# Parameter rows on ScalarE's queue, x without a pause on SyncE's, and two dense steps between the last transposes of x

## The reference

```
def rmsnorm(x, g):
    y = x * rsqrt(mean(x * x, axis=-1) + EPS)
    return y * g

for i in range(DEPTH):                      # 2 layers
    h = rmsnorm(x, norm_g[i])
    proj = einsum('bsd,dn->bsn', h, w_in[i])
    (qa, ka, va, fa, za, qb, kcb, ...) = split_cols(proj)
    ...                                     # three mixers, merge, residual, embedding
return rmsnorm(x, final_g)
```

## Time and profile before

| | |
|---|---|
| median of three runs | 1510.43 us (1510.29 to 1510.44) |
| profiled execution, its own time | 1511.0 us |
| its span, first to last instruction | 1509.1 us |
| mean granted TensorE clock | 0.995 |
| PE busy | 1477.2 us, 98% of the span |
| DVE busy | 938.5 us, 62% |
| ACT busy | 634.6 us, 42% |

### The profile page before, as it was taken

One profiled execution on the slowest core, in us unless ns is written; L12 is line 12 of the kernel. 1 busy time (PEld: TensorE's weight loads), 2 busy tenths in 40 slices (PEclk: granted clock), 3 DMA queues, 4 the chain that ended last, 5 costly groups with the idle time before them and its releaser, 6 DMA issues.

```text
span 1509.1 us, 22243 instructions
## 1 busy us (share of the span) xinstructions
PE 1477.2 (98%) x7765; PEld 1226.0 (81%) x7765; DVE 938.5 (62%) x2197; ACT 634.6 (42%) x1499; POOL 75.8 (5%) x79
## 2 busy tenths in 40 slices
PE   7999999999999999999999999999999999999997
PEld 6777788888888887888787887888888888878885
DVE  5866765655657776454576667655555666855544
ACT  5544434434344344243444434334344444434343
POOL 1000000000001000000100000000000000000011
PEclk9999999999999999999999999999999999999998
DMA  6325353224325543332342345423343355433222
GB/s 188 85 80 124 107 123 78 71 71 112 78 64 139 140 119 85 110 102 70 109 110 70 104 100 129 116 57 78 79 99 82 98 126 127 111 99 104 84 88 74
DMA packets 259262, 150.48 MB, mean 100 GB/s; under 512 B 47482, under 2 KB 247764, under 8 KB 259156
## 3 DMA queue, kind: packets, MB, share of 16 engines
q1 hardware_dynamic: 259156, 149.11, 38.1%
HBM read 118.67 MB, written 2.10 MB: 80 GB/s over the span
## 4 chain that ended last, share of the span: by engine, by line
PE 82%; DVE 8%; ACT 3%; issue 3%; DMA 2%; SPq 1%; POOL 0%; ACTq 0%; POOLq 0%; DVEq 0%
PE D L774 22%; PE D L776 21%; PE D L775 21%; PE Ob L965 7%; PE T L943 4%; DVE w_lo L1329 3%; PE S L930 2%; PE S L931 2%; ACT w_hi L1095 1%; PE S L920 1%; DMA arena<-rcs 1%; PE Mb L981 1%; ACT probs L1207 1%; DVE v_b L1424 1%; PE Ob L969 1%
## 5 line engine op out<-in xcount | busy, mean ns | idle before, releaser
L774 PE MATMUL D<-h_hi,w_hi 128*128 128x512 f32 x1264 | 539.0, 426 | 3.5 <-DVE w_lo L1329 1.7
L1329 DVE TENSOR_TENSOR w_lo<-raw,w_hi 128x512 fp32r<-128x512 f32 (+2 forms) x504 | 296.3, 628 | 322.8 <-ACT w_hi L1095 322.5
L776 PE MATMUL D<-h_lo,w_hi 128*128 128x512 f32 x1264 | 496.9, 393 | 0.0
L775 PE MATMUL D<-h_hi,w_lo 128*128 128x512 f32 x1264 | 494.9, 392 | 0.0
L1095 ACT ACTIVATE w_hi<-raw 128x512 fp32r<-128x512 f32 (+2 forms) x504 | 263.6, 569 | 291.4 <-PE D L776 287.9
L776 PEld LDWEIGHTS D<-h_lo,w_hi 128*128 128x128 f32 x1264 | 237.6, 188 | 53.4
L1207 ACT ACTIVATE probs<-probs,nmax 128x128 f32<-128x128 f32 (+3 forms) x256 | 141.9, 555 | 330.0 <-DVE nmax L1580 329.9
L774 PEld LDWEIGHTS D<-h_hi,w_hi 128*128 128x128 f32 x1264 | 239.2, 189 | 47.5 <-issue 6.6
L775 PEld LDWEIGHTS D<-h_hi,w_lo 128*128 128x128 f32 x1264 | 239.9, 190 | 30.4 <-issue 0.5
L1580 DVE CUSTOM_DVE_ANT_0 probs<-S,maskb 128x128 f32<-128x128 f32 (+3 forms) x256 | 115.2, 487 | 26.2 <-PE S L923 12.8
L556 DVE COPY pT<-T 128x128 f32<-128x128 f32 (+3 forms) x160 | 77.6, 487 | 55.1 <-PE T L943 54.5
(11 more groups left out here) (249 smaller groups left out, 1596.2 us busy)
## 6 DMA issues: line engine op xcount, KB each, us to landing
raw<-in_w_in_dram SPq DMA_DIRECT2D x124, 512.0 KB, 4.0
arena<-rcs SPq DMA_DIRECT2D x48, 256.0 KB, 4.4
raw<-in_w_in_dram SPq DMA_DIRECT2D x32, 256.0 KB, 3.7
arena<-rcs SPq DMA_DIRECT2D x64, 128.0 KB, 2.3
raw<-in_w_out_dram SPq DMA_DIRECT2D x16, 512.0 KB, 4.1
raw<-in_w_ple_gate_dram SPq DMA_DIRECT2D x16, 512.0 KB, 4.1
rcs<-rx SPq DMA_DIRECT2D x80, 64.0 KB, 2.0
raw<-in_cmp_w_k_dram SPq DMA_DIRECT2D x8, 512.0 KB, 3.7
```

What stands on the lines that cost most here:

```text
L774: pe.matmul(o, w_hi[:, sl, cs], hi[:, k, :], start=(k == 0), stop=False)
L775: pe.matmul(o, w_lo[:, sl, cs], hi[:, k, :], start=False, stop=False)
L776: ins = pe.matmul(o, w_hi[:, sl, cs], lo[:, k, :], start=False, stop=last)
L1329: TT(w_lo[:, sl, half], raw[:, ring(L, t, RAW), half], f(w_hi[:, sl, half]), ALU.subtract).then_inc(M["dve_lo"], 1)
```

## The change

Three edits, all of them ahead of or in the first tile of the first layer:

- The five parameter loads leave SP's queue and become the first instructions of ACT's. SP's queue then goes from `x_part(0)` straight to `x_part(1)`, the weights of tile 0, and the rest as before.
- The loop over the eight transposed blocks moves on PE to just ahead of the tiles (nothing stood between).
- Ahead of the transposes of block 6 PE runs step 0 of tile 0 (`va` 0), and ahead of those of block 7 step 1, each behind a wait for the first half of `w_lo` of tile 0 and for `h_lo` of its block. These two steps are left out where they stood.

```
--- before.py
+++ after.py
+        EARLY = 2
...
             @block.sync
             def _(sp):
-                rows_ = [(norm_g.rearrange("a (m p) -> (a m) p", p=P), 0, PAR_PK),
-                         (cmp_pe_k.rearrange("a (m two) d -> (a m) (two d)", two=2), PAR_PK, 16 * DEPTH),
-                         (cmp_pe_v.rearrange("a (m two) d -> (a m) (two d)", two=2), PAR_PV, 16 * DEPTH),
-                         (diff_subln_g, PAR_SUB, DEPTH),
-                         (final_g.rearrange("(m p) -> m p", p=P), PAR_FIN, NM)]
...
                 x_part(0)
-                for src, r, n in rows_:
-                    sp.dma_start(prow[r:r + n, :], src).then_inc(i_par, 16)
                 for L in range(DEPTH):
...
                 pe.transpose(Ob[:, 0:PAR], prow, ident[0:PAR, 0:PAR]).then_inc(i_pe, 1)
-                for m in range(NM):
...
                 for L in range(DEPTH):
...
+                    if L == 0:
+                        for m in range(NM):
+                            if m >= NM - EARLY:
+                                pe.wait_ge(M["dve_lo"], 1)
+                                pe.wait_ge(M["h_lo_s"], m - (NM - EARLY) + 1)
+                                dense("va", 0, m - (NM - EARLY))
+                            if m % (NM // XQ) == 0:
+                                pe.wait_ge(i_x[m // (NM // XQ)], 16)
+                            if m == 5:
+                                pe.wait_ge(i_gain, 1)
+                            if m == 6:
+                                pe.wait_ge(i_dve, 1)
+                            if m == 7:
+                                pe.wait_ge(i_xa, 1)
+                            for t in range(NQ):
+                                ins = pe.transpose(first_banks[m % 6][:, t * P:(t + 1) * P], x_tok[:, t, m * P:(m + 1) * P], ident[:])
+                            ins.then_inc(i_pe, 1)
+
                     for it in items:
                         what = it[0]
                         if what == "mm":
                             t, k = it[1:]
                             kind, n, _ = tiles[t]
+                            if L == 0 and t == 0 and k < EARLY:
+                                continue
...
             @block.scalar
             def _(act):
                 A = act.activation
...
+                for src, r, n in rows_:
+                    act.dma_start(prow[r:r + n, :], src).then_inc(i_par, 16)
                 act.wait_ge(i_const, 3)
                 A(nrm[:, 3, 0:1], ones[:], ACT.Square).then_inc(i_act, 1)
```

More of the change, by code:

```diff
@@ L1076, in _ @@
                 A = act.activation
+                rows_ = [(norm_g.rearrange("a (m p) -> (a m) p", p=P), 0, PAR_PK),
+                         (cmp_pe_k.rearrange("a (m two) d -> (a m) (two d)", two=2), PAR_PK, 16 * DEPTH),
+                         (cmp_pe_v.rearrange("a (m two) d -> (a m) (two d)", two=2), PAR_PV, 16 * DEPTH),
+                         (diff_subln_g, PAR_SUB, DEPTH),
+                         (final_g.rearrange("(m p) -> m p", p=P), PAR_FIN, NM)]
+                for src, r, n in rows_:
+                    act.dma_start(prow[r:r + n, :], src).then_inc(i_par, 16)
                 act.wait_ge(i_const, 3)
```

## The result

The changed kernel is slower: 1512.27 us in the median of 22 runs (1510.36 to 1514.02), against 1509.71 us for the kernel before in 22 runs beside them (1508.40 to 1511.04). The ratio is 1.0014, with a 95% interval of 1.0008 to 1.0020: about 2.1 us more, 1.2 to 3.0 (the two medians alone lie 2.6 apart). The forecast was 1507.1, in a range up to 1509.8, so sign and range were both wrong. By its own bound of 0.2% the outcome is in the class to which the prediction gave 0.60, within 0.2%; with 22 runs on either side even a smaller loss can be told from none. The larger sample also moves the base: the profiled execution that the sum was made against took 1511.0 us, 1.3 more than this median.

The account below looks back on a forecast made before the run. The prediction took PE to bound the kernel, busy for 1477.2 of 1509.1 us. From the profiled 1511.0 us it took 3.3 gained at tile 2, then 0.6 for the lower median: 1507.1 us, range 1506.5 to 1509.8.

Parts of the forecast that it names:

- I take about 5.3, since the rows are on a queue without bulk loads but share the engines: At the start: the last parameter row, issued on ACT, lands at about 5.3 us; the worst row near it would make 8.1.
- the third rival: At the start: bulk loads hold up the parameter rows until 8.1 us; kernel 0.3 us slower, 1510.8; chance 0.08.
- the sum is made against its own time: Whole kernel: 1511.0 us of one profiled execution, less 3.3, is 1507.7; the median is 0.6 lower, so 1507.1.
- The forecast gain of 3.3 us at tile 2: First layer: tile 2 starts at 24.75 instead of 28.07 us, and the gain passes to the kernel's end.
- no stretch under 300 GB/s: Transfers between 2.5 and 10 us: the hole at 102 GB/s closes, so loads land 1.1 us sooner.
- the second rival: At the start: x and weights land no sooner, only issuing time is saved; gain 0.7 us, 1509.7; chance 0.15.
- The chain behind block 7: From block 7's end to tile 2's weights on ACT and DVE: 11.2 us, not shortened by the change.
- The wait at the vt transposes: PE, ahead of tile 2: it waits about a microsecond for ACT's evacuation of tile 0.
- `lo(4)` moved with `lo(3)`: DVE's low weights of tiles 3 and 4: `lo(3)` comes 3.3 to 3.4 us sooner, and what follows moves with it.
- Part 2, the steps,: PE around block 6: steps 0 and 1 run early at the high clock; block 7 ends 1.35 us sooner, at 13.55.
- theory C: Posed after the measurement: the moved steps hold back block 7, on which the chain to tile 2 hangs; no chance given.
- A: Posed after the measurement: rows on ACT's queue wait for bulk loads, so PE starts 2.84 us late; no chance given.

Follow-up runs that it names:

- e7: The changed kernel with SP's loads from `x_part(1)` on held back until the parameter rows have landed; 1514.14 us in a single run.
- e11: The changed kernel with `norm_g` and both `cmp_pe` rows on ACT's queue, the other two on SP's behind `x_part(0)`, early steps kept; 1509.24 us, single run.
- e9: The changed kernel without early steps, PE's first wait for `norm_g` alone, all rows transposed behind block 7; 1509.43 us, ratio 0.9998 to the kernel before.
- e13: The kernel before, unaltered, run once more for another profile; 1508.94 us in a single run.
- e14: The kernel before, unaltered, run once more for another profile; 1508.79 us in a single run.
- after: The profiled execution of the changed kernel itself; it took 1512.32 us.
- e1: The changed kernel without the two early steps, all rows still on ACT's queue; 1511.20 us, ratio 1.0011 to the kernel before.
- e15: The same as e11 but without the two early steps; 1508.94 us, ratio 0.9999 to the kernel before.
- e2: The changed kernel with the rows back on SP's queue between `x_part(0)` and `x_part(1)`, early steps kept; 1509.10 us, ratio 1.0001 to the kernel before.
- e4: The changed kernel with all rows on SP's queue behind `x_part(1)`, early steps kept; 1509.91 us, ratio 1.0002 to the kernel before.
- e6: The same as e5 but with both early steps; 1509.81 us, ratio 1.0004 to the kernel before.
- e10: The same as e9 but with both early steps; 1510.13 us, ratio 1.0004 to the kernel before.
- e5: The changed kernel with only both `cmp_pe` rows on ACT's queue, three on SP's behind `x_part(0)`, no early steps; 1509.89 us, ratio 1.0005 to the kernel before.
- e12: The changed kernel, unaltered, run again for a second profile; 1511.93 us in a single run.

## Why the prediction was wrong

**The step that failed: "I take about 5.3, since the rows are on a queue without bulk loads but share the engines".** They landed at 8.1, the upper bound that stood beside it. The bound came from a small load that had to pass bulk loads on SP's own queue; I took the second queue to spare that. Turns were taken, but the pulses of queue 10 lie about a whole 512 KB load apart, and PE started 2.84 us later than in the earlier trace rows. e7 (no bulk beside them: 5.34), e11 (three rows: 5.45) and e9 (the first row: 3.58) bear that out.

The Trainium skill, which I had beside it ("DMA: Bandwidth & Descriptors", section "Queues, rings and completion order"), has each DMA engine take turns between queues a whole packet at a time, and a packet there is a batch of descriptors, typically 9 to 17 and at most 64. If a record of the profile is one descriptor, 512 KB in records of 1 KB are 32 for each of sixteen engines, an estimate: pulses a whole load apart are longer than the typical packet and inside the limit. So I had read into the page that the turns would be short; it does not say so, and the measurement shows that they were long.

**What followed was the third rival, worked out rightly.** It put the end of `h_hi` 1 near 11.0 (measured 9.55 + 1.48 = 11.03) and the copy of block 0 at 14.2 (13.68 + 0.61 = 14.29). Of its path only the last step, blocks 6 and 7 at the low clock until 17.2, was too late, for the clock rose at 12.3 and stayed up: 16.17. It had a chance of 0.08, and its condition, a landing behind 7.8, was met.

**The second failure: "the sum is made against its own time".** The base was one execution in which tile 0 ran at the low clock. The forecast gain of 3.3 us at tile 2, 28.07 to 24.75, was mostly that stretch; against the 25.39 of e13 and e14 the same 24.75 is a gain of 0.6, less than 0.05% of the time. And the rival's price of 0.3 us was worked out against the same base; against e13 and e14 the measured end of block 7, 16.17, is 2.1 us late (13.98 and 14.20). Nothing in the one profile said that its clock could go otherwise; that its time lay above the median of the three runs hinted at it.

**What held.**
- SP and the transfers: forecast a gain of 1.1 us, and "no stretch under 300 GB/s" from 2.5 us on; measured 280, 382 and 322 in the windows from 2.5 to 6.5, and 313 and 348 in those up to 8 and 10, short only in the first. Weights of tile 0 landed at 1.78 + 6.5 = 8.3 (forecast 8.5); that is 1.3 us sooner than in the first profile, but only 0.5 sooner than in e13 and e14, where they were issued at 3.83, as in the first profile, but took 5.0 and 4.9 us. The Trainium skill's rule that issuing from several engines saves only the sequencer's time, usually little beside the transfer ("DMA: Bandwidth & Descriptors", section "Issuing engines are not separate DMA queues"), read as in the second rival, would have left the hole. Here the traces show it filled, because the saved issues stood ahead of bulk loads while the engines ran dry. The rule's other half, that loads from all engines interleave on the same sixteen engines, agrees with the late rows.
- The chain behind block 7: forecast 11.2 us to tile 2's weights; tile 2 starts 27.47 - 16.17 = 11.3 behind it in after, and 11.3 in e13 and e14 as well (25.27 - 13.98, 25.51 - 14.20).
- The wait at the vt transposes: forecast about 1 us for ACT; measured 1.08. `lo(4)` moved with `lo(3)`, though not by the 3.3 us forecast: they begin 0.77 and 0.47 us sooner than in the earlier trace rows, while `lo(2)` begins 1.28 us later, at 26.73.
- The issues on ACT cost nothing: it idles 4.70 us before its first `h_hi`.

**Part 2, the steps,** ran at the high clock as forecast, by luck: the forecast had the clock up long before, and it rose at 12.3, half a microsecond ahead of step 0. But what they save PE buys nothing while the chain behind block 7 sets tile 2. Step 1 stands between blocks 6 and 7 in the way of that chain: block 7 ends at 16.17 with it and 15.49 without (e1), tile 2 0.3 to 0.5 us later; 0.8 us later in e11 than in e15; not later in e2 than in e13 and e14. By the times the early steps' price is not to be told from none (1.0014 beside 1.0011, 1.0004 beside 0.9998, all intervals overlapping). So theory C holds in some of the traces, with some tenths of a microsecond, and A carries the result. From the traces the rows' share of the loss at tile 2 is 26.93 - 25.39 = 1.54 us and the steps' 27.37 - 26.93 = 0.44, if e13 and e14 are taken for the kernel before; with one or two traces of each kernel that split is rough.

The clock shows one thing more of the steps. Both profiles of the kernel before in which it fell behind 12 us have a mean granted clock of 0.995, as do 22 of 89 runs of that kernel beside the experiments; of the 66 runs of the change, e2, e4, e6 and e10, all with both early steps, none has. But e1, without the steps, has none in 11 either. That the steps keep the clock from falling is not shown by this, and the times show no gain from it.

No version beats the kernel before: the best, e9 and e15, are level with it at 0.9998 and 0.9999, and of the 0.5 to 3 us that I had expected e2, e4, e5 and e9 to gain on it nothing came. With the rows in time the loads of x and the weights come sooner, and yet block 7 ends at 13.34 (e9) to 14.42 (e15), beside 13.98 and 14.20.

**Open:** what of the loss lies behind tile 2, if any; and why the clock rises at 8.7 in one execution of the kernel before and near 13.7 in another, with PE started at 5.2 to 5.4 in both and the same transposes behind it.

## What to carry to other kernels

A small load that an engine waits for at its start belongs ahead of the bulk loads in time, not merely on another queue: here each further load on the second queue waited for about one more 512 KB load, as long as such loads stood next in the first. If it must go beside bulk, let the first wait ask only for the row that is needed first, as e9 does: it left the queues as in the change, and no loss remained that the times show. And before pricing an edit in the first microseconds, look at more than one execution of the kernel before: a stretch at the low clock in a single profile can make a gain that other runs don't have, and two executions picked by their times can make a loss look better explained than it is.

## What the hardware showed that was not expected

- Two queues appear to share the DMA engines by whole loads: with five small loads beside 512 KB ones, queue 10 moved 32, 48, 64 and 4 packets in pulses that began at 2.2, 4.2, 5.7 and 7.2 us, though the last load was issued at 3.04.
- The granted clock at the start of an unchanged kernel has more than one course: up at 8.7, down at 12.1, up at 18.9; down from 12.6 to 16.0; or up once near 13.7 (two profiles). The own times were 1511.0, 1511.06, and 1508.94 and 1508.79 us. The column of the granted clock reads 1.00 from 5.0 to 6.5 us in the earlier trace rows, where the transposes take 421 ns just as those of the earlier trace rows do, so ahead of its first change the durations are the better witness.
- PE waited for a transfer into the arena near 514 us for 1.52 us (after) and 1.56 us (e9), and not at all in e12, which is the same program as after.
- The granted clock falls near the end of the kernel in every trace, at 1495.1 us in e13 at the earliest and at 1500.5 in after at the latest of the six traces of the two kernels.
